# Mixture-of-experts layer of a decoder step: expert rows kept in a table in HBM and fetched per token, in place of scatter products

## The reference, cut to what matters

```
logits = h @ w_router
top_v, top_i = top_k(logits, 2)
wts = softmax(top_v)
gate = sum over the two of one_hot(top_i, 8) * wts
for e in range(8):
    acc += gate[..., e] * ((silu(h @ wg[e]) * (h @ wu[e])) @ wd[e])
x = x + acc
y = rmsnorm(x, norm_final)
```

## Time and profile before

| | |
|---|---|
| median of 3 runs | 1508.69 us (1507.61 to 1509.31) |
| profiled execution, its own time | 1509.33 us |
| its span | 1507.5 us |
| TensorE busy | 1468.9 us, 97% of the span |
| VectorE, ScalarE, GpSimd busy | 313.3, 184.2, 35.4 us |
| moved by DMA | 475.66 MB |
| mean granted clock of TensorE | 0.989 |

### The profile page before, as it was taken

One profiled execution on the slowest core, in us unless ns is written; L12 is line 12 of the kernel. 1 busy time (PEld: TensorE's weight loads), 2 busy tenths in 40 slices (PEclk: granted clock), 3 DMA queues, 4 the chain that ended last, 5 costly groups with the idle time before them and its releaser, 6 DMA issues.

```text
span 1507.5 us, 31559 instructions
## 1 busy us (share of the span) xinstructions
PE 1468.9 (97%) x13941; PEld 850.1 (56%) x13941; DVE 313.3 (21%) x772; ACT 184.2 (12%) x462; POOL 35.4 (2%) x54
## 2 busy tenths in 40 slices
PE   9999999999998999999998999999998999999997
PEld 7887787878875557535435336335344345336444
DVE  4222223233246881300010110000010110110011
ACT  3000000001023661100000000000000000000001
POOL 3000000001000001000000000000000000000000
PEclk9999999999999999999999999999999999999899
DMA  9966665436435555899999999999999999999893
GB/s 340 346 267 239 251 252 183 163 133 215 158 100 176 169 119 245 303 378 393 404 409 424 425 407 424 423 348 371 424 408 425 427 408 410 409 365 378 346 427 128
DMA packets 95184, 475.66 MB, mean 316 GB/s; under 512 B 9984, under 2 KB 35760, under 8 KB 70207
## 3 DMA queue, kind: packets, MB, share of 16 engines
q1 hardware_dynamic: 92999, 467.92, 79.3%
q0 software_dynamic: 2048, 5.72, 1.2%
HBM read 469.73 MB, written 12.71 MB: 320 GB/s over the span
## 4 chain that ended last, share of the span: by engine, by line
PE 87%; DMA 8%; SPq 2%; DVE 1%; ACT 1%; issue 1%; DVEq 0%; ACTq 0%
PE banks L1163 34%; PE banks L1228 14%; PE banks L773 11%; PE banks L791 6%; PE banks L840 5%; DMA ring<-in_w_moe_gate 3%; DMA arena<-in_cache_kv 3%; PE banks L1264 2%; PE banks L1111 2%; PE banks L918 2%; PE banks L1038 1%; PE banks L754 1%; PE banks L1173 1%; PE banks L1138 1%; PE banks L935 1%; DMA ring<-in_state_win 1%
## 5 line engine op out<-in xcount | busy, mean ns | idle before, releaser
L1163 PE MATMUL banks<-ring,arena 128*32 128x512 f32 (+1 forms) x5376 | 523.9, 543 | 4.4 <-DMA ring<-in_w_moe_gate 3.6
L1163 PEld LDWEIGHTS banks<-ring,arena 128*32 128x32 f32 x5376 | 168.3, 110 | 329.8 <-issue 326.9
L1228 PE MATMUL banks<-ring,arena 128*32 128x256 f32 x4704 | 259.0, 379 | 7.0 <-DMA ring<-in_w_moe_down 3.3
L1228 PEld LDWEIGHTS banks<-ring,arena 128*32 128x32 f32 x4704 | 154.1, 110 | 105.0 <-DMA ring<-in_w_moe_down 5.8
L773 PE MATMUL banks<-hT,ring 128*128 128x264 f32 x896 | 204.0, 389 | 0.0
L773 PEld LDWEIGHTS banks<-hT,ring 128*128 128x128 f32 x896 | 170.3, 191 | 37.6 <-issue 8.7
L1969 DVE TENSOR_TENSOR xT<-banks,xT 128x264 f32<-128x264 f32 x56 | 24.2, 433 | 504.3 <-PE banks L1264 504.3
L791 PE MATMUL banks<-arena,ring 128*128 128x264 f32 x448 | 101.4, 387 | 0.0
L791 PEld LDWEIGHTS banks<-arena,ring 128*128 128x128 f32 x448 | 84.6, 190 | 19.2 <-issue 5.0
L840 PE MATMUL banks<-hT,ring 128*128 128x264 f32 x256 | 57.4, 386 | 0.0
L1988 DVE TENSOR_TENSOR arena<-arena,banks 128x512 f32<-128x512 f32 (+1 forms) x42 | 24.2, 617 | 146.7 <-PE banks L1163 146.7
(11 more groups left out here) (316 smaller groups left out, 885.2 us busy)
## 6 DMA issues: line engine op xcount, KB each, us to landing
ring<-in_w_moe_gate SPq DMA_DIRECT2D x64, 1792.0 KB, 16.3
ring<-in_w_moe_up SPq DMA_DIRECT2D x64, 1792.0 KB, 14.8
ring<-in_w_moe_down SPq DMA_DIRECT2D x32, 2048.0 KB, 17.8
ring<-in_w_moe_down SPq DMA_DIRECT2D x32, 1536.0 KB, 18.2
arena<-in_cache_kv SPq DMA_DIRECT2D x64, 256.0 KB, 8.0
ring<-in_cache_kv SPq DMA_DIRECT2D x128, 128.0 KB, 2.2
ring<-in_w_ffn_gate SPq DMA_DIRECT2D x7, 2048.0 KB, 10.8
ring<-in_w_ffn_up SPq DMA_DIRECT2D x7, 2048.0 KB, 13.0
```

What stands on the lines that cost most here:

```text
L1163: last = mm(banks[CT * q:CT * (q + 1), 2 * t + part, 0:PART_W[part]], xe[:, c, CT * t:CT * (t + 1)], w[:, at:at + PART_W[part]], start=(c ...
L1228: last = mm(banks[CT * q:CT * (q + 1), 6 + place // 2, 256 * (place % 2):256 * (place % 2 + 1)], mh[:, t, at:at + CT], w[:, r, 256 * h:256 ...
```

## The change

1. The scatter products of items 0 to 6 are gone, with Gm, GT, ynat and the additions to xT for them. ScalarE copies the output rows of an item to `yst`, GpSimd stores them to a table `y_rows` in HBM (one DMA for two tiles, a second for the third tile), with row 0 all zero.
2. `find_rows` on VectorE, in item 0, computes for each token the two rows of that table that belong to it (`tok_rows`).
3. The residual stream is turned to token rows (`x_rows`) after down chunk 6 of items 1 and 4, and kept in `rows_acc`.
4. After item 6, GpSimd waits for all stores and fetches for each third of the tokens its two rows (88 rows each) with two indirect DMAs into `y_got` and `xg`; VectorE adds them with their weights to `rows_acc`. There are three such rounds on the same two buffers.
5. The loop item's rows come from the table h_rows, fetched during item 6, in place of the gather at the loop's start. Inside the loop item, the rows for a next loop item are gathered after up chunk 4, whether there is a next one or not.
6. Inside the loop item, `add_over` after up chunk 1 adds the rows of the loop item before it (with this count GT is zero), with six products and six VectorE additions to rows_acc; `sum_rows` puts rows_acc into PSUM in the down stage in place of `rows_of_x`.
7. Parts reordered: a chunk takes part 0 of all tiles and then part 1; silu, multiplication, transposes and copies go by part. The down stage starts with part 0 turned, and part 1 is turned after down chunk 0. `turn_rows` moves from after down chunk 3 to after chunk 5.

```diff
+            def store_rows(i, nt):
+                base = 1 + CT * sum(ITEM_TILES[:i])
+                gp.wait_ge(yn_sb, i + 1)
+                gp.dma_start(y_rows[base:base + 2 * CT].rearrange("r (b c) -> b r c", b=2), yst[:, 0:512]
+                             ).then_inc(stored, 16)
+                if nt == 3:
+                    gp.dma_start(y_rows[base + 2 * CT:base + 3 * CT].rearrange("r (q c) -> q r c", q=4), yst[:, 512:768]
+                                 ).then_inc(stored, 16)
+            gp.wait_ge(rows_added, 1)
+            gp.dma_start(y_rows[0:1], y_got[0:1, :]).then_inc(stored, 16)
+            for i in range(LOOP0):
                 fetch_rows(i, ITEM_TILES[i + 1])
+                store_rows(i, ITEM_TILES[i])
+            gp.wait_ge(stored, rows_stored(LOOP0))
+            gp.wait_ge(xe_ps, LOOP0 + 1)
+            for j in range(NTC):
+                for k, dst in enumerate((y_got, xg)):
+                    if j:
+                        gp.wait_ge(rows_added, 2 * j + k)
+                    gp.indirect_dma_start(out=dst[0:TT, :], out_offset=None, in_=y_rows,
+                                          in_offset=bass.IndirectOffsetOnAxis(ap=tok_rows[0:TT, NTC * k + j:NTC * k + j + 1], axis=0)
+                                          ).then_inc(xg_in, 16)
+            gp.wait_ge(rows_added, 1 + 2 * NTC)
+            gp.dma_start(y_got[0:TT, :], bc(norm_final, 0, TT)).then_inc(xg_in, 16)
...
+            def chunk(i, kind, c, nt):
+                wait_expert_tile(pe, i, kind, c)
+                for part in range(2):
                     for t in range(nt):
+                        if kind == UP and c == 0:
+                            pe.wait_ge(msilu, parts_before(i) + (part * nt + t + 1))
+                        last = products(kind, c, part, t, expert_view(kind, c))
...
+            def item(i, nt, after):
+                pe.wait_ge(xe_sb, i * 2 + 2)
...
+                for c in range(NC):
+                    chunk(i, GATE, c, nt)
+                for c in range(NC):
+                    chunk(i, UP, c, nt)
+                    if c == 2:
+                        if i:
+                            pe.wait_ge(yn_sb, i)
+                        next_rows(i, after)
+                turn_hidden(i, 0, nt)
+                pe.wait_ge(rows_sb, i + 1)
+                pe.wait_ge(mt_sb, parts_before(i) + nt)
                 for k in range(NK):
+                    if k == 4:
+                        pe.wait_ge(mt_sb, parts_before(i) + 2 * nt)
+                    down_products(i, k, nt)
+                    if k == 0:
+                        turn_hidden(i, 1, nt)
+                    if k == 5:
                         turn_rows(i, after)
+                    if k == 6 and i == 1:
+                        x_rows((0, 1, 2, 3))
+                    if k == 6 and i == 4:
+                        x_rows((4, 5))
...
+            def add_over(i):
+                pe.wait_ge(gt_sb, i * 1)
+                pe.wait_ge(yn_sb, i * 1)
+                for w in range(6):
+                    j, hf = divmod(w, 2)
+                    if w >= 4:
+                        pe.wait_ge(so_added, i * 6 + (w - 3 - 6 * LOOP0))
+                    mm(banks[0:TT, 4 + w % 4, :], GT[0:CT * LT, j * TT:(j + 1) * TT],
+                       ynat[0:CT * LT, 512 * hf:512 * (hf + 1)], start=True, stop=True).then_inc(so_ps, 1)
...
+            def last_item(i):
+                pe.wait_ge(xe_sb, i * 2 + 2)
+                for c in range(NC):
+                    chunk(i, GATE, c, LT)
+                for c in range(NC):
+                    chunk(i, UP, c, LT)
+                    if c == 1:
+                        add_over(i)
+                    if c == 3:
+                        pe.wait_ge(so_added, i * 6 + (6 - 6 * LOOP0))
+                        pe.wait_ge(G_ready, i + (1 - LOOP0))
...
+                    if c == 4:
+                        pe.wait_ge(P_ready, i + 2)
+                        gather(LT)
+                turn_hidden(i, 0, LT)
...
+                    if k == 1:
+                        pe.wait_ge(xe_sb, i * 2 + 4)
+                        sum_rows(4)
+                        sum_rows(5)
+                    if k in (2, 3):
+                        sum_rows(2 * k - 4)
+                        sum_rows(2 * k - 3)
...
 # VectorE
+            V.memset(GT[0:CT * LT, :], 0.0).then_inc(gt_sb, LOOP0)
+            dve.wait_ge(xn_act, 11)
+            for j in range(NTC):
+                dve.wait_ge(xg_in, 16 * (LOOP0 + 2 * j + 2))
+                for k, got in enumerate((y_got, xg)):
+                    dve.wait_ge(rows_added, 1 + 2 * j + k)
+                    stt(rows_acc[j][R, :], got[R, :], top[:, 15 + 3 * k + j:16 + 3 * k + j], rows_acc[j][R, :], ALU.mult, ALU.add
+                        ).then_inc(rows_added, 1)
+            dve.wait_ge(rows_added, 1 + 2 * NTC)
             count = dve.value_load(n_items[0:1, 0:1], min_val=NE, max_val=MAXI)
             with dve.Fori(LOOP0, count) as i:
+                last_item(i)
```

More of the change, by code:

```diff
@@ L1155, in _ @@
             gather(ITEM_TILES[0])
[L1156 to L1164, removed]
-                return last
@@ L1167, in turn_hidden, with products @@
-            def turn_hidden(i, t):
-                pe.wait_ge(mhid, tiles_before(i) + (t + 1))
-                for part in range(2):
+            def products(kind, c, part, t, w):
+                for q in range(4):
+                    at = PART_AT[part] + PART_W[part] * q
+                    last = mm(banks[CT * q:CT * (q + 1), 2 * t + part, 0:PART_W[part]], xe[:, c, CT * t:CT * (t + 1)],
+                              w[:, at:at + PART_W[part]], start=(c == 0), stop=(c == NC - 1), skip_group_check=True)
+                return last
@@ L1274, in item, with x_rows @@
-            def item(i, first, nt, before, after):
-                if not isinstance(i, int):
-                    pe.wait_ge(mt_sb, tiles_before(i))
-                    pe.wait_ge(P_ready, i + 1)
-                    gather(nt)
-                gate_stage(i, first, nt, before)
-                up_stage(i, first, nt, after)
-                down_stage(i, nt, after)
+                last.then_inc(tile_used, 1)
+            def x_rows(ws):
+                for n, w in enumerate(ws):
+                    j, hf = divmod(w, 2)
+                    for c in range(4):
+                        last = tr(banks[0:TT, n, c * P:(c + 1) * P], xT[:, 4 * hf + c, j * TT:(j + 1) * TT], ident)
+                last.then_inc(xn_ps, 1)
@@ L1468, in item @@
                     last = nc.scalar.copy(ynat[0:64, 512 * hf:512 * (hf + 1)], banks[64 * hf:64 * (hf + 1), 6, :])
[L1469 to L1472 removed]
                 last.then_inc(yn_sb, 1)
             for i in range(LOOP0):
[L1476 removed]
+                item(i, ITEM_TILES[i], ITEM_TILES[i + 1])
             act.wait_ge(table_ready, 1)
@@ new lines, in item, with multiply @@
+            def item(i, nt, after):
+                places(code_of(i + 1), after)
+                if i == 0:
+                    find_rows()
+                multiply(i, nt)
+            def multiply(i, nt):
+                for part in range(2):
+                    a = PART_W[0] * part
+                    for t in range(nt):
+                        if part == 0 or t < nt - 1:
+                            dve.wait_ge(mgu_ps, products_before(i) + (2 * nt - 1 + part * nt + t + 1))
+                        else:
+                            dve.wait_ge(tile_used, used(i, UP, NK - 1))
+                        tt(msg[:, t, a:a + PART_W[part]], msg[:, t, a:a + PART_W[part]],
+                           banks[:, 2 * t + part, 0:PART_W[part]], ALU.mult).then_inc(mhid, 1)
```

331 lines of the change are left out of this document (164 added, 167 removed).

## The result

The changed kernel takes 1543.13 us (median of 4 runs, 1542.3 to 1544.7) against 1508.55 us, a ratio of 1.0236 with the interval 1.0219 to 1.0254. The direction was forecast, the size was not: +34.6 us in place of +16, and above the range.

The account below looks back on a forecast made before the run. TensorE and DMA were taken to be in balance: 14 us gained before the loop item, 99.4 us in it and a 33 us wait put its end 16 us later, 1524.5 us in all. Range 1514 to 1541; 8 in 10, 1499 to 1540.

Parts of the forecast that it names:

- What bounds the kernel: Items 1 to 6: TensorE and the weight transfers by DMA are in balance, with little slack on either side.
- What DMA lets through: Before the loop item: of 35 us saved on TensorE, 14 come out, bounds 8 and 19.
- The loop item without the stop: TensorE's time from the loop item's start to the last six products, if nothing waits: 99.4 us, against 102.5 before.
- The new wait: In add_over TensorE waits 33 us for VectorE's additions, behind copies, stores and three fetch rounds; bounds 3 and 42.
- T0: The start of the loop item, forecast at 1378.8 in place of 1392.8.
- the landing of the stores: After item 6, GpSimd's two stores take 10 us to land, within bounds of 5.5 and 16.
- The fetches: Three rounds after item 6: 16.6 us per pair of 88-row fetches, 18 per round, with 3 us relief in round three.
- The formula of the Trainium skill: A GpSimd DMA takes about 2.0 us plus its bytes at 436 GB/s; by it the stall would be nothing.
- After the loop item: What follows the start of the last six products is unchanged.
- The sum: Start of the last six products: 1392.8 - 14 + 99.4 + 33 = 1511.2, 16 us later than before.
- Rival 1: The loop item's fetch chain is short or hidden, so the kernel takes 1491.6 us; chance 0.22, with the cases between.
- Rival 3: DMA was the bound all along: only 5 us come out of items 1 to 6, 1534 to 1543 us; chance 0.15.

Follow-up runs that it names:

- run 5: Changed kernel without the six last fetches, their six additions and the stores of the experts' rows: 1483.3 us, ratio 0.9854.
- run 4: Changed kernel without the six last fetches and their six additions, stores kept: 1494.9 us, ratio 0.9926.
- Run 1: Changed kernel with an item's rows stored by plain two-dimensional copies in place of copies with a split row: 1536.2 us, ratio 1.0210.
- Run 3: Changed kernel with the wait for the stores taken out and the six last fetches reading h_rows, stores kept: 1537.3 us, ratio 1.0209.
- run 6: Changed kernel with only items 0 to 5 in the table, item 6 kept as a product with GT, and the fetch rounds during item 6: 1509.7 us.
- run 7: Changed kernel with fetch rounds during item 6, item 6 kept as a product with GT, and plain two-dimensional stores: 1505.0 us, ratio 0.9989.
- run 2: Changed kernel with the same stores, in the same shape, issued from ScalarE's queue in place of GpSimd's: 1566.7 us, ratio 1.0397.
- run 9: Kernel before the change with two more copies of each of its six row fetches, into SBUF that nothing reads: 1518.4 us, ratio 1.0083.

## Why the prediction was right or wrong

- **What bounds the kernel:** right. DMA is full in items 1 to 6 (share 1.00 to 1.01), and TensorE waits for it in items 1, 2, 4 and 5. Items 3 and 6 have nothing to wait for and take 113.7 us, for which the sum had 114.4.
- **What DMA lets through:** right, and nearer than 17.7 us against 14 suggests. 3.0 of the 17.7 lie ahead of item 0. From item 1's start to the loop item it is 658.7 us before and 644.4 after, 14.3 less. The stores' 5 us were about right too: leaving them out gave 5.7 us from item 0 to the loop item (run 5).
- **The loop item without the stop:** 99.4 forecast; 153.2 - 49.4 = 103.8 in the changed kernel and 102.6 in run 4. The sum took waits for weights at nothing; there were 3.0 us of them ahead of add_over (0.9, 1.3 and 0.8), and 3.7 in run 4.
- **The new wait:** its place, its releaser and its chain are as described, and its size was wrong: 49.4 us, not 33. The chain ran to T0 + 86.7 (T0 is 1375.1), not 67, and TensorE, which had waited for weights, arrived at T0 + 37, not 34. By links: copies, stores and landing 31.6 us against 12.3; three rounds 51.1 against 52.3; places and first addition 4.1 against 3. **The step that failed is the landing of the stores, which I took at 10 us and which was 29.** Its nearest rows, 5.5 and 10.0 us, were copies of whole rows, one of them with little beside it, and even the upper bound of 16 counted one packet per partition. The prediction's 256 packets were 672, most of them tiny. Run 1 has the same bytes landed in 13.8 us with 224 packets, so the shape of the store makes more than half of the time. Run 3 shows that the packets delay the fetches behind them even where nobody waits for the store.
- **The fetches:** 0.059 us per row gave 16.6 us per pair; measured 19.7 and 18.2 us, and 7.4 for the third, which I had only partly relieved. The two errors cancel, so that the 51.1 us for the rounds are near the 52.3 by luck.
- **The formula of the Trainium skill** ("DMA: Bandwidth & Descriptors", anatomy of one DMA) gives an estimate of some 4 us per pair: the first pair took 19.7 us beside a full ring, almost five times that. With the weights through, 7.4 us per pair came nearer. The same page's section on queues, rings and completion order says that an engine takes turns between queue rows by packets. Run 1 fits that, with fewer packets landing sooner; that a packet of the page is one of the profile's is not shown.
- **After the loop item:** the last stretch took 14.5 us where 12.25 was carried over. Its six products ran mostly at 1.2 GHz (granted 0.58) and took 8.3 us, not 5.35. That the tail is unchanged was wrong by 2.2 us. It is not the stop's doing: they took 8.6 us in run 4, without a stop, and 5.35 in run 1, with one of 40.9.
- **The sum,** in span: -17.7 + (103.8 - 102.45) + 49.4 + 2.2 = +35.3, as measured. Against the forecast the stop gives 16.4 us of the miss, the rest of the loop item 4.4, the tail 2.2. The earlier start of the loop item takes 3.7 off, 3.0 of them by luck. The rivals: none came true alone. Rival 1's case exists (run 4, 1494.9), but the fetches would have to cost nothing. Rival 3's time came true (1543), but not its mechanism: 14 us and not 5 came out of items 1 to 6, and what the stores cost beyond their bytes was their landing in the chain.

What follows from the runs about the change as a whole: it takes work from TensorE and gives DMA 2.5 MB of stores, which cost the weights 5.7 us (run 5), and 2.2 MB of fetches, which cost more than three times their bytes, 17 to 19 us where they meet the weights (run 6). Even with the chain hidden (run 7) it only comes out even.

## What to carry to other kernels

Where an engine is 97% busy and DMA full in the same stretches, cost a change in both; work taken from the one is worth only the other's slack. Price a small transfer beside a full ring from a row of such a transfer in such a stretch, and twice: what it takes to land, and what it takes from the stream beside it. Before a store goes on a chain that TensorE ends in, look at its packets: the same bytes as plain two-dimensional copies landed in less than half the time. And before two traces are compared at one point, compare them where both kernels still do the same work: here that took 3 us off a gain of 17.7.

## What the runs showed of the hardware that I had not expected

- A store of 128 partitions of 2 KB with a split destination, from GpSimd, landed in 24.6 to 25.1 us beside the weights in all seven cases; with it and its smaller companion item 6's 0.39 MB were 672 packets and took 30.3 us, as two plain stores and four small ones 224 packets and 13.8 us.
- The same stores from ScalarE's queue took about 57 us for item 6 (run 2).
- A fetch of 88 to 96 rows of 4 KB costs the weight stream an estimated 2.7 to 3.2 us, against 0.9 for its bytes, with the share of busy DMA unchanged (runs 6 and 9). Its 4 KB packets take 0.21 us each; the weights' 14 KB packets beside them take 0.73 us, and 0.54 without them (run 6).
- A fetch issued behind a store in GpSimd's queue lands after it, though no semaphore orders them (run 3).
